# Beginning the transfers that regroup attention weights on POOL's queue, both ways together

## The chip, the cores and the metric

The kernel runs on one core of one Trainium2 chip. The metric is the device time of one execution in microseconds; the time of the kernel before is the median of three runs. One further execution was profiled, and every row of a trace below comes from that one.

## What is computed

Two transformer blocks of width 1024 are applied one after the other to 512 tokens, all in float32. The first has two layers, each with three attentions side by side: `forgetting_attention` (A, 4 heads), `dilated_mixture_attention` (B, 6 heads) and a banded attention with sinks (C, 6 query heads, 2 key heads). The second has two layers as well. The first of them holds the differential attention with a relative bias, and both hold a cross attention to 256 memory rows and an MLP.

```python
def reference(x, norm_g, w_in, ..., mlp_w2_2):
    x = first_block(x, norm_g, w_in, b_forget, sinks, w_br_a, w_br_b, w_br_c, w_out, final_norm_g)
    return second_block(x, mem_2, rel_bias_2, ...)

# the differential attention, whose weights are regrouped as those of A, B and C are
a = probs(qa, k1) - lam * probs(qc, k2)
return jnp.einsum('bhqk,bkhd->bqhd', a.astype(v.dtype), v)

# the cross attention of a layer
p = jax.nn.softmax(s, axis=-1)
o = jnp.einsum('bhsm,bmhd->bshd', p.astype(h.dtype), kv[:, :, 1]).reshape(B, S, D_MODEL)
```

## The kernel before, in words

`schedule` writes one list of steps for the whole program. Each of five functions, one per engine, walks that list and issues what of it belongs to its engine. So the place of a step in the list is its place in every engine's queue, and there is no other scheduler. Semaphores tie the engines together.

**Products.** Each float32 product is taken as three fp32r products of high and low parts (`tensor_program`, L2118 to L2120). The weights come from HBM in pieces of up to 128x1040 into a ring of four buffers `t_raw` (the step `fetch`, L2063, issued by SP). ACT rounds a piece to `t_whi` (L2261, four buffers), and DVE takes the rest to `t_wlo` (L2434, three buffers). The fetch of piece j+4 waits until DVE has made the low part of piece j, since it overwrites that piece's buffer.

**Attention.** `attention` works through units, each two heads (or one head's two maps) by 128 or 256 queries. Matmuls of the projections that come next (`gens_B`, `gens_C`, `gens_D`, `fill_E`, `fill`) are drawn in between by `drive`, in a fixed ratio. A unit goes: scores on PE (L2135), mask and maximum on DVE, exponents on ACT, division and write of the weights into a block by ACT (L2362, L2398) or, in the differential attention, by DVE (L2694); then the regrouping; then the values on PE (L2146). The weights have queries on the partitions, and the values need keys there.

**The regrouping** is made of three steps. `far_out` (L2079) writes the block to the HBM scratch `far` in one DMA, 128 partitions by 4 pieces. `far_in` (L2085) reads it back in four DMAs, each filling 32 partitions with 4 pieces. `turn_near` (L2701) then transposes 32x32 squares on DVE. One such journey, out and back, will be called a **trip**. There are 42 in A, B and C of the two layers (`t_Tb`), 12 in the differential attention (`t_UP`), and 8 in the first cross attention (`t_E`); 310 DMAs in all. Two scratch buffers alternate (`w` is 0 or 1): the way out waits until the trip two before it has landed in full (`back`). The way back waits until the way out has landed, and for a free buffer. The block is a ring of one buffer, so the next unit's weights cannot be written before the way out has landed.

**SP's queue.** All DMAs are issued by SP (`sync_program`), one after the other in the order of the list: the fetches of weights, the trips, and the swaps of halves for the rotary embedding (L2074). A waiting instruction holds up all that is behind it. `send_away` puts `far_out` in the list one `flush` after the weights, and `come` puts `far_in` one `flush` further, so that fetches and swaps come to stand between them.

**POOL's queue** (`gpsimd_program`) holds only the ten window sums of the pooling (L2101), which all lie between the last trip of block one and the first of the differential attention.

Of the kernel before, what the change touches and what calls it, by code (L numbers as in the profile page):

```python
# [95 lines left out]
class Signals:  # L96
# [5 lines left out]
    def mark(self, name, n=0, by=1):  # L102
        sem = SEMAPHORE.get(name, name)
        self.count[sem] = self.count.get(sem, 0) + by
        self.value[name, n] = self.count[sem]
        return sem, by

    def at(self, name, n=0):
        return name, 0
# [49 lines left out]
def schedule(T, A, plan, apart=()):  # L159
# [5 lines left out]
    def emit(name, **f):  # L165
        n = ids[name] = ids.get(name, -1) + 1
        s = Rec(f, name=name, id=n)
        steps.append(s)
        return s
# [20 lines left out]
    def gcol(name, t=0):  # L190
        return gv[:, GV[name] + t:GV[name] + t + 1]
# [14 lines left out]
    if not dry:  # L206
        at = 0
# [153 lines left out]
    def later(f, n=1):  # L361
        late.append(f if n == 1 else lambda: later(f, n - 1))
# [202 lines left out]
    def send_away(u):  # L565
        n = u["tiles"]
        src, ready = u["far"]
        w, k = moved[0] % 2, moved[0] // 2
        moved[0] += 1
        far = A["far"][w][:, :, 0:32 * n]  # L570

        def go():
            emit("far_out", w=w, k=k, dst=far.rearrange("j p c -> p j c"),
                 src=src[:, 0:128 * n].rearrange("p (j c) -> p j c", j=4), after=ready, back=back[w])
            blocks.give(src, (f"far{w}", k))
            later(come)

        def come():
            dst, free = grouped.take()
            emit("far_in", w=w, k=k, free=free,  # L580
                 pairs=[(dst[32 * j:32 * j + 32, 0:128 * n].rearrange("p (i c) -> p i c", i=4),
                         far[j].rearrange("(i a) c -> a i c", i=4)) for j in range(4)])
            back[w] = f"near{w}", (k, 3)
            u["near"] = dst, back[w]

        later(go)
# [270 lines left out]
    for m in range(8):  # L857
        s = emit("norm_hi", dst=P0.hi[:, m, :], src=X[:, m, :], col=gcol("norm0", m), after=c_x[m], gain=c_gv)
# [1193 lines left out]
def sync_program(e, steps, at, mark):  # L2052

    sent = 0
    for s in steps:
        if s.name == "load":
            for k in s.after:
                e.wait_ge(*at(*k))
            e.dma_start(s.dst, s.src).then_inc(*mark(f"load{s.n}", by=16))
        elif s.name == "fetch":  # L2060
            for k in s.after:
                e.wait_ge(*at(*k))
            e.dma_start(s.dst, s.src).then_inc(*mark(f"raw{s.j % NRAW}", s.j, by=16))  # L2063
        elif s.name == "fetch_cut":
            e.dma_start(s.dst, s.src).then_inc(*mark(f"cut{s.j}{s.k}", by=16))
        elif s.name == "rope":
            e.wait_ge(*at("rope_sin", s.n))
            for k in s.bfree:
                e.wait_ge(*at(*k))
            if s.before is not None:  # L2070
                e.wait_ge(*at(*s.before))
            for q in range(4):
                to, of = 32 * (q ^ 1), 32 * q
                e.dma_start(s.b[to:to + 32, :], s.u[of:of + 32, :]).then_inc(*mark(f"swap{s.n % 3}", (s.n, q), by=16))  # L2074
        elif s.name == "far_out":
            e.wait_ge(*at(*s.after))
            if s.back is not None:
                e.wait_ge(*at(*s.back))
            e.dma_start(s.dst, s.src).then_inc(*mark(f"far{s.w}", s.k, by=16))  # L2079
        elif s.name == "far_in":  # L2080
            e.wait_ge(*at(f"far{s.w}", s.k))
            for k in s.free:
                e.wait_ge(*at(*k))
            for j, (dst, src) in enumerate(s.pairs):
                e.dma_start(dst, src).then_inc(*mark(f"near{s.w}", (s.k, j), by=16))  # L2085
        elif s.name == "send":
            e.wait_ge(*at("scaled", s.id))
            e.dma_start(s.dst, s.x).then_inc(*mark("sent", s.id, by=16))
            sent = s.id
    e.wait_ge(*at("sent", sent))  # L2090


def gpsimd_program(e, steps, at, mark):

    for s in steps:
        if s.name == "pool_in":
            e.wait_ge(*at("pool_in", s.g))
            for i, (dst, a, b) in enumerate(s.adds):
                if i:
                    e.wait_ge(*at("window", (s.g, i - 1)))  # L2100
                e.tensor_tensor(dst, a, b, ALU.add).then_inc(*mark("window", (s.g, i)))  # L2101


def tensor_program(e, steps, at, mark, T):
# [839 lines left out]
def build_program(nc, A, pack):  # L2944
    from contextlib import ExitStack

    with ExitStack() as ctx:
# [9 lines left out]
        for program in (sync_program, gpsimd_program):  # L2957
            program(Counting(), steps, signals.at, signals.mark)
# [12 lines left out]
        @block.sync  # L2971
        def _(e):
            sync_program(e, steps, at, mark)
# [9 lines left out]
        @block.gpsimd  # L2983
        def _(e):
            gpsimd_program(e, steps, at, mark)
# [96 lines left out]
```

## Time and profile before

| | |
|---|---|
| median of three runs | 2223.2 us (2221.88 to 2223.98) |
| profiled execution, its own time | 2222.34 us |
| its span in the trace | 2220.3 us |
| TensorE matmul busy | 2199.0 us, 99% of the span |
| DVE busy | 1454.9 us, 66% |
| ACT busy | 975.7 us, 44% |
| POOL busy | 14.5 us, 1% |
| 16 DMA engines, mean share | 39% |

A busy PE here means that a matmul was under way by the trace; matmuls are pipelined, and one with 512 columns starts every 0.23 us. Times in the trace count from the start of the span. Stretches that matter: block one's attentions from 60 to 310 us and from 480 to 745 us, the differential attention from 925 to 1025 us, the first cross attention from 1090 to 1180 us.

### The profile page before, as it was taken

What the parts mean: (1) busy time and instruction counts of PE and PEld (TensorE: products, weight loads), DVE (VectorE), ACT (ScalarE), POOL (GpSimd) and SP (SyncE); (2) the same over time, 40 slices, a digit from 0 to 9 for tenths busy, and PEclk for the clock granted to TensorE, in tenths of its full rate; (3) what the DMA queues carried; (4) which work ended last, traced back from release to release, by engine and by line L of the source; (5) the groups of instructions that cost most, each with busy time, mean ns of one, the idle gap of its engine ahead of it and who ended that gap; (6) DMA issues with size and microseconds to landing.
All of it is one profiled execution on the core that took longest, in us unless ns stands there. A gap on an engine that the chain in (4) does not pass through costs nothing.

```text
span 2220.3 us, 31738 instructions
## 1 busy us (share of the span) xinstructions
PE 2199.0 (99%) x12112; PEld 1860.7 (84%) x12112; DVE 1454.9 (66%) x2448; ACT 975.7 (44%) x1676; POOL 14.5 (1%) x14
## 2 busy tenths in 40 slices
PE   9999999999999999999999999999999999999998
PEld 7877788888778888888898889998888888899997
DVE  5866565557656567686665777776755657776775
ACT  5445533334445334364553544443322435444444
POOL 0000000000000000200000000000000000000000
PEclk9999999999999999999999999999999999999999
DMA  5565443335644333465354333333233213233331
GB/s 201 164 186 156 146 129 109 104 125 180 185 135 152 116 101 115 125 176 147 114 154 132 95 95 96 114 96 105 88 99 96 89 48 105 88 102 97 99 112 55
DMA packets 136694, 268.14 MB, mean 121 GB/s; under 512 B 21773, under 2 KB 79931, under 8 KB 136160
## 3 DMA queue, kind: packets, MB, share of 16 engines
q1 hardware_dynamic: 136544, 266.13, 39.3%
q8 instruction: 96, 1.57, 0.3%
q14 instruction: 54, 0.44, 0.1%
HBM read 235.37 MB, written 26.77 MB: 118 GB/s over the span
## 4 chain that ended last, share of the span: by engine, by line
PE 70%; DVE 3%; ACT 1%; issue 1%; DMA 1%; POOL 1%; SPq 0%; DVEq 0%; POOLq 0%; ACTq 0%
PE ps L2118 22%; PE ps L2120 22%; PE ps L2119 22%; PE ps L2146 1%; PE ps L2135 1%; DVE t_wlo L2434 1%; POOL t_UP L2101 1%; DMA far<-t_UP 0%; DVE t_UP L2694 0%; PE ps L2170 0%; DVE t_Tb L2662 0%; PE ps L2158 0%; PE ps L2160 0%; PE ps L2159 0%; PE ps L2172 0%
## 5 line engine op out<-in xcount | busy, mean ns | idle before, releaser
L2118 PE MATMUL ps<-t_P0H,t_whi 128*128 128x512 f32 (+1 forms) x1568 | 590.6, 377 | 3.8 <-DVE t_P0L L2479 1.9
L2119 PE MATMUL ps<-t_P0L,t_whi 128*128 128x512 f32 (+1 forms) x1568 | 584.4, 373 | 0.0
L2120 PE MATMUL ps<-t_P0H,t_wlo 128*128 128x512 f32 (+1 forms) x1464 | 552.8, 378 | 0.0
L2434 DVE TENSOR_TENSOR t_wlo<-t_raw,t_whi 128x1024 fp32r<-128x1024 f32 (+2 forms) x289 | 342.7, 1186 | 44.7 <-PE ps L2120 32.2
L2261 ACT ACTIVATE t_whi<-t_raw 128x1024 fp32r<-128x1024 f32 (+2 forms) x295 | 300.8, 1025 | 153.6 <-PE ps L2120 152.1
L2118 PEld LDWEIGHTS ps<-t_P0H,t_whi 128*128 128x128 f32 x1568 | 295.2, 188 | 73.1 <-issue 16.4
L2119 PEld LDWEIGHTS ps<-t_P0L,t_whi 128*128 128x128 f32 x1568 | 294.9, 188 | 56.2 <-issue 1.0
L2120 PEld LDWEIGHTS ps<-t_P0H,t_wlo 128*128 128x128 f32 x1464 | 275.2, 188 | 54.7
L2118 PE MATMUL ps<-t_P1H,t_whi 128*128 128x512 f32 (+1 forms) x548 | 210.0, 383 | 1.6 <-DVE t_P1L L2819 1.0
L2119 PE MATMUL ps<-t_P1L,t_whi 128*128 128x512 f32 (+1 forms) x548 | 208.5, 380 | 0.0
L2120 PE MATMUL ps<-t_P1H,t_wlo 128*128 128x512 f32 (+1 forms) x524 | 201.1, 384 | 0.0
L2119 PE MATMUL ps<-t_P1L,t_MH 128*128 128x512 f32 x384 | 150.7, 393 | 0.0
L2120 PE MATMUL ps<-t_P1H,t_ML 128*128 128x512 f32 x384 | 150.6, 392 | 0.0
L2118 PE MATMUL ps<-t_P1H,t_MH 128*128 128x512 f32 x384 | 150.2, 391 | 0.0
L2831 DVE TENSOR_TENSOR t_X<-ps,t_X 128x512 f32<-128x512 f32 (+1 forms) x136 | 88.8, 655 | 74.0 <-PE ps L2120 73.9
L2268 ACT ACTIVATE t_whi<-t_raw 128x1024 fp32r<-128x1024 f32 x72 | 75.8, 1055 | 109.4 <-DVE t_raw L2449 109.4
L2118 PEld LDWEIGHTS ps<-t_P1H,t_whi 128*128 128x128 f32 x548 | 103.2, 188 | 22.9 <-DVE t_P1L L2819 1.2
L2119 PEld LDWEIGHTS ps<-t_P1L,t_whi 128*128 128x128 f32 x548 | 103.1, 188 | 20.8 <-issue 0.2
L2120 PEld LDWEIGHTS ps<-t_P1H,t_wlo 128*128 128x128 f32 x524 | 98.4, 188 | 20.9
L2414 ACT ACTIVATE t_TMP<-t_TMP 128x512 f32<-128x512 f32 x64 | 40.2, 628 | 136.6 <-DVE t_TMP L2827 136.6
L2287 ACT ACTIVATE t_P0H<-t_X,t_gv 128x512 fp32r<-128x512 f32 x56 | 40.3, 725 | 113.7 <-DVE t_X L2600 100.7
L2342 ACT ACTIVATE t_Tb<-t_Tb,t_ST 128x128 f32<-128x128 f32 (+3 forms) x96 | 51.6, 539 | 86.7 <-DVE t_ST L2670 73.0
(348 smaller groups left out, 3880.4 us busy)
## 6 DMA issues: line engine op xcount, KB each, us to landing
t_raw<-in_wts SPq DMA_DIRECT2D x362, 512.0 KB, 3.6
far<-t_Tb SPq DMA_DIRECT2D x26, 384.0 KB, 3.1
far<-t_Tb SPq DMA_DIRECT2D x16, 512.0 KB, 3.4
t_PTX<-far SPq DMA_DIRECT2D x64, 96.0 KB, 3.5
t_raw<-in_wts SPq DMA_DIRECT2D x16, 384.0 KB, 3.2
t_QKV<-far SPq DMA_DIRECT2D x32, 128.0 KB, 2.8
t_raw<-in_wts SPq DMA_DIRECT2D x13, 256.0 KB, 2.8
t_PTX<-far SPq DMA_DIRECT2D x24, 128.0 KB, 4.0
```

Of the source, the lines that this page charges most:

```text
L2101: e.tensor_tensor(dst, a, b, ALU.add).then_inc(*mark("window", (s.g, i)))
L2118: e.matmul(s.out, s.sh, s.mh, start=s.first, stop=False, skip_group_check=again)
L2119: e.matmul(s.out, s.sh, s.ml, start=False, stop=False, skip_group_check=again)
L2120: i = e.matmul(s.out, s.sl, s.mh, start=False, stop=s.end, skip_group_check=again)
L2135: i = e.matmul(bank[:, o:o + n], q, k, start=True, stop=True)
L2261: e.activation(s.dst, s.raw, ACT.Copy).then_inc(*mark("hi", s.j))
L2268: e.activation(s.hi, s.src, ACT.Copy).then_inc(*mark("part_hi", s.id))
L2287: e.activation(s.dst, s.src, ACT.Copy, scale=s.col).then_inc(*mark("norm_hi", s.id))
L2342: i = e.activation(t[:, o:o + n], t[:, o:o + n], ACT.Exp, bias=s.s[:, 4 + c + k:5 + c + k], accum_out=s.s[:, 8 + c + k:9 + c + k])
L2414: e.activation(s.t, s.t, ACT.Square).then_inc(*mark("relu_square", s.id))
L2434: e.tensor_tensor(s.dst, s.raw, s.hi.bitcast(F32), ALU.subtract).then_inc(*mark("lo", s.j))
L2831: e.tensor_tensor(s.x, s.bank, s.x, ALU.add).then_inc(*mark("add_x", s.id))
```

## The change

The two steps of a trip move from `sync_program` to `gpsimd_program`, and `come` is called at once where it was put off by a `flush`, so that the way back stands directly behind the way out in the list. Nothing else is changed; PE, DVE and ACT have the same instructions in the same order.

```diff
             blocks.give(src, (f"far{w}", k))
-            later(come)
+            come()
@@ def sync_program
-        elif s.name == "far_out":
-            e.wait_ge(*at(*s.after))
-            if s.back is not None:
...
+def gpsimd_program(e, steps, at, mark):
+
+    for s in steps:
+        if s.name == "pool_in":
...
+        elif s.name == "far_out":
+            e.wait_ge(*at(*s.after))
+            if s.back is not None:
+                e.wait_ge(*at(*s.back))
+            e.dma_start(s.dst, s.src).then_inc(*mark(f"far{s.w}", s.k, by=16))
+        elif s.name == "far_in":
+            e.wait_ge(*at(f"far{s.w}", s.k))
+            for k in s.free:
+                e.wait_ge(*at(*k))
+            for j, (dst, src) in enumerate(s.pairs):
+                e.dma_start(dst, src).then_inc(*mark(f"near{s.w}", (s.k, j), by=16))
```

SP's queue at the start of the differential attention, before (a row is one instruction, or several alike with their count: line, DMA, what is written from what, the shape):

```order
L2063 DMA t_raw<-in_wts 128x1024 x3
L2079 DMA far<-t_UP 128x4x96
L2063 DMA t_raw<-in_wts 128x1024
L2085 DMA t_UP<-far 32x4x96 x4
L2079 DMA far<-t_UP 128x4x96
L2085 DMA t_UP<-far 32x4x96 x4
L2063 DMA t_raw<-in_wts 128x1024
L2079 DMA far<-t_UP 128x4x128
L2063 DMA t_raw<-in_wts 128x1024
L2085 DMA t_UP<-far 32x4x128 x4
```

In the changed kernel SP's queue has only fetches there (thirteen in a row), and these rows stand on POOL, behind the window sums:

```order
+L2090 TENSOR_TENSOR t_UP<-t_UP 128x512 x10
+L2095 DMA far<-t_UP 128x4x96
+L2101 DMA t_UP<-far 32x4x96 x4
+L2095 DMA far<-t_UP 128x4x96
+L2101 DMA t_UP<-far 32x4x96 x4
+L2095 DMA far<-t_UP 128x4x128
+L2101 DMA t_UP<-far 32x4x128 x4
```

So a trip is held up by no fetch any more and holds up none, and a way out stands behind the whole trip before it. In the changed kernel L2095 is the way out, L2101 the way back and L2090 the window sums.

## Rows read from the trace of the kernel before

**Rows 1.** The page's first part: busy time of each engine
```profile
span 2220.3 us, 31738 instructions
PE 2199.0 (99%) x12112; PEld 1860.7 (84%) x12112; DVE 1454.9 (66%) x2448; ACT 975.7 (44%) x1676; POOL 14.5 (1%) x14
```

**Rows 2.** Busy time by stretches of the program; the last columns are clock, DMA share, GB/s
```profile
60.00:125.00 65.00, 62.31 (x403) 52.51 (x403) 51.03 (x95) 26.35 (x54) 0.00 (x0) 1.00 0.59 178
925.00:1025.00 100.00, 94.88 (x701) 85.71 (x700) 79.45 (x227) 61.26 (x123) 0.00 (x0) 1.00 0.59 169
1090.00:1180.00 90.00, 89.94 (x642) 84.26 (x641) 56.54 (x92) 47.73 (x90) 0.00 (x0) 1.00 0.52 153
```

**Rows 3.** Who waited for whom, 925 to 1025 us: total us, times, longest
```profile
DVE t_UP L2694 <- DMA far<-t_UP: 4.0, 2, 2.0
PE ps L2146 <- DVE t_E L2778: 2.8, 2, 1.7
PE ps L2118 <- DVE t_wlo L2434: 1.9, 1, 1.9
DVE t_PTb L2701 <- DMA t_UP<-far: 0.8, 1, 0.8
```

**Rows 4.** The chain that ended last, 925 to 1025 us: start, us, what
```profile
929.94 3.32 DMA far<-t_UP
...
937.64 0.58 DVE t_PTb L2701
...
941.78 1.24 DVE t_wlo L2434
943.15 0.47 PE ps L2118
```

**Rows 5.** Way out L2079, then way back L2085, 925 to 1025 us: ns of issue; landing
```profile
L2079 SPq DMA_DIRECT2D far<-t_UP x12: 370/382/383, 929.9 to 1010.0; - x12
DMA to landing us min/median/max: 2.2/3.1/5.7
...
L2085 SPq DMA_DIRECT2D t_UP<-far x48: 302/432/441, 933.3 to 1014.2; - x48
DMA to landing us min/median/max: 1.7/2.5/3.8
```

**Rows 6.** POOL's own work, L2101, whole span: ns min/median/max
```profile
L2101 POOL TENSOR_TENSOR t_UP<-t_UP x10: 1040/1156/1952, 898.6 to 922.0; 128x512 f32<-128x512 f32 x10
```

**Rows 7.** Way back L2085, whole span: ns of issue, min/median/max
```profile
L2085 SPq DMA_DIRECT2D t_E<-far x32: 313/432/2001, 1097.9 to 1170.1; - x32
```

**Rows 8.** Timeline: ACT's last write of a block (L2362), DVE's turn (L2701)
```profile
533.80 0.71 ACT L2362 ACTIVATE t_Tb<-t_TbX,t_ST 128x512 f32<-128x512 f32 x1
543.33 1.25 DVE L2701 STREAM_TRANSPOSE t_M<-t_M 128x1024 f32<-128x1024 f32 x1 [1.54 <-DMA t_M<-far]
```

**Rows 9.** The same two steps (L2398, L2701) of the last cross attention trip
```profile
1163.02 0.91 ACT L2398 ACTIVATE t_E<-t_Tb,t_ST 128x256 f32<-128x256 f32 x2 [1.24 <-DVE t_ST L2804]
1172.19 0.71 DVE L2701 STREAM_TRANSPOSE t_PTb<-t_E 128x512 f32<-128x512 f32 x1 [4.33 <-DMA t_E<-far]
```

**Rows 10.** Timeline 925 to 950 us: DVE's write of the block, then SP's queue
```profile
939.17 1.14 DVE L2694 SCALAR_TENSOR_TENSOR t_UP<-t_Tb,t_ST 128x128 f32<-128x128 f32 x4 [0.63 <-ACT t_Tb L2352]
948.03 0.88 DVE L2694 SCALAR_TENSOR_TENSOR t_UP<-t_Tb,t_ST 128x128 f32<-128x128 f32 x3 [2.04 <-DMA far<-t_UP]
943.03 0.35 SPq L2063 DMA_DIRECT2D t_raw<-in_wts  x1
943.48 0.38 SPq L2079 DMA_DIRECT2D far<-t_UP  x1
```

**Rows 11.** SP's waits, whole span: total us, times, longest; and ACT's for a fetched piece (L2261)
```profile
SPq L2079 <- ACT t_Tb L2362: 71.5, 28, 6.5
SPq L2085 <- DMA far<-t_Tb: 42.3, 22, 3.8
...
  DMA t_raw<-in_wts: 1.3, 3
```

More of the change, by code:

```diff
@@ L2074, in sync_program @@
                 e.dma_start(s.b[to:to + 32, :], s.u[of:of + 32, :]).then_inc(*mark(f"swap{s.n % 3}", (s.n, q), by=16))
-        elif s.name == "far_out":
-            e.wait_ge(*at(*s.after))
-            if s.back is not None:
[L2078 to L2085, printed above, removed]
         elif s.name == "send":
```

## The prediction

> **What bounds the kernel now.** I read the page's first part, then busy time by stretches, then the waits and the chain inside the stretches that hold trips. PE is busy for 2199.0 of 2220.3 us [rows 1], and it runs the same matmuls after the change. So all a faster trip can give is some of PE's idle time there: 2.7 us between 60 and 125 us, 5.1 us between 925 and 1025 us, and 0.1 us between 1090 and 1180 us [rows 2]. What can be lost has no such limit. A trip that lands late stops DVE at the turn, and DVE also makes the low parts of the weights for PE. The place to look at is the differential attention, since DVE is busy there for 79.5 of 100 us [rows 2] and has little room to catch up. PE's stalls there end with DVE's work: 2.8 us on values and 1.9 us on a low part [rows 3]. Just before that 1.9 us the chain runs way out (3.32 us), way back, turn [rows 4]: this first trip is on the path already, for its turn waits 0.8 us for the landing [rows 3].
>
> **What goes away.** (1) SP loses 310 issues. They stood beside other work. SP waited 71.5 us for weights to be written and 42.3 us for ways out to land [rows 11] with fetches queued behind it, but ACT waited for a fetched piece only three times, 1.3 us in all [rows 11]. Freed fetches are covered by the four-buffer ring; I count nothing. (2) A trip no longer queues behind a fetch. The clearest case: DVE has written a block at 939.17 + 1.14 = 940.3 us, but SP issues it at 943.48, right behind a fetch issued at 943.03. DVE then waits 2.04 us for that way out to land before it may write the next block [rows 10]. On POOL the issue can be 3.2 us earlier. I count **-2.0 us**.
>
> **What is added.** POOL must issue one DMA out and four back per trip. No row shows a DMA issued by POOL, so its price is bounded. Below: SP's issue, 0.38 us out and 0.43 us back [rows 5]. Above, for the way back: the longest single issue that SP shows, 2.0 us [rows 7]. Above, for the way out: its whole time from issue to landing, 3.1 us [rows 5], as if writing out the transfer's parts took as long as moving them. For the way back I take 1.04 us, POOL's shortest instruction on a full tile [rows 6], the nearest row of that engine. The way out has 512 runs of memory (128 x 4) against 128 in a piece of the way back (32 x 4), so I take the middle of its two ends, (0.38 + 3.1) / 2 = 1.75 us.
>
> The rest of a landing: the shortest way out landed 2.2 us after its issue began [rows 5], 1.8 without the issue; I take 1.9. For the way back the median is 2.5 us, less 0.43 makes 2.1; with pieces spaced further apart I take 2.0. A trip from block written to landed is then 1.75 + 1.9 + 4 x 1.04 + 2.0 = **9.8 us**, and it holds POOL's queue for all but the last 2.0, **7.8 us**, as the way back waits in the queue for the way out.
>
> The Trainium skill ("DMA: Bandwidth & Descriptors", Latency and other measured facts) puts the first byte of a POOL transfer at about 1 us and that of an SP transfer at about 0.6 us. By these figures alone the two legs would lose some 0.8 us a trip; no run so far shows it.
>
> **Where 9.8 us is late.** From the block written to the turn there are now:
> - first trip of the differential attention: 929.9 to 937.64, 7.7 us [rows 4]. Late by **2.1 us**, in full, since it is on the path.
> - last forgetting trip of layer two: 534.5 to 543.33, 8.8 us [rows 8]; its twin of layer one, read the same way, 9.5 us. Late by 1.0 and 0.3 us, 1.3 in all. I count half, **0.6 us**, DVE being busy there for 51.0 of 65 us [rows 2].
> - last cross attention trip: 1163.9 to 1172.19, 8.3 us [rows 9], late by 1.5; two more of its eight, read the same way, have 8.9 and 9.1 us and are late by 0.9 and 0.7. DVE's wait of 4.33 us there [rows 9] goes with 0.1 us lost on PE [rows 2]. Of 3.1 us I count half, **1.6 us**.
> - the other 57 trips, read the same way, have 10 to 23 us and are covered; if POOL's cost eats that cover, the heavy rival below holds.
>
> **The queue itself.** The 12 ways out of the differential attention are issued from 929.9 to 1010.0 us [rows 5], one per 7.28 us. A trip would hold POOL for 7.8 us. So POOL becomes the slowest stage there, and each of the 11 intervals grows by 0.5: **+5.7 us**. In the cross attention the cadence is (1164.0 - 1095.3) / 7 = 9.8 us, the first and last way out being those of its eight trips, and in block one's attentions it is longer still, so nothing piles up there. POOL's window sums end before 925 us [rows 2, 6] and collide with nothing.
>
> Sum: -2.0 + 2.1 + 0.6 + 1.6 + 5.7 = +8.0 us. I add 1 us for trips of the differential attention between the first and the last whose room is 10 to 12 us and which start behind a late one: **+9 us**. The profiled execution took 2222.34 us, so the next would take 2231.3; the median of the runs stands 0.9 higher, which gives **2232 us** for it. What a measurement here can tell from no change is about 0.2%, 4.4 us.
>
> **Rivals.**
> 1. *Hidden.* If POOL issues either way for at most 0.7 us, a trip takes 0.7 + 1.9 + 2.8 + 2.0 = 7.4 us, under the tightest 7.7, and holds POOL for 5.4 of 7.28 us. Nothing is late and the -2.0 stands: 2221 us, no change that can be told. For it: PE is 99% busy [rows 1] and most trips have much room. Against: a software path on an engine whose shortest full tile instruction takes 1.04 us [rows 6]. The Trainium skill (same page, Anatomy of one DMA) says that a DMA issued by POOL costs about 2.0 us plus 1 us per 436,000 bytes, and that writing its descriptors is a small part. By that rule a way out of 192 KB would land after an estimated 2.5 us and the overlapping ways back in little over 2.1 us, and this rival would win; the page is the main thing that speaks for it. 22%.
> 2. *Faster.* The same cheap issue, and the freed order also gives PE back its stalls: the 1.9 us on a low part, behind which stands the trip chain, and the 2.8 us on values [rows 3]. 2223.2 - 4.7 = 2218.5 us. It decides where a trip lands before 7.7 us and SP's fetches in front of it were what held DVE. Against: DVE's 79.5% [rows 2] stays, and only one of these waits leads back to a trip. 11%.
> 3. *Heavy.* The way out costs POOL its upper bound, 3.1 us. A trip is then 11.2 us and holds POOL for 9.2: in the differential attention 11 x (9.2 - 7.28) = 21 us and 3.5 for the first trip, in the cross attention 2.9 late at the last trip and some 6 over the others, in block one 1.7 + 2.7 at the two tight trips, in all some 37 less 2: 2258 us. With 1.5 us for each way back as well it would pass 2300. The Trainium skill ("SBUF — State Buffer", Who interferes with whom) adds a way to it: POOL writes descriptors through a port that some DVE instructions lock. No row here shows such a lock. 27%.
> 4. *Nothing happens*, since waits tie the trips to the same moments. The queues do change, and the 3.2 us behind a fetch [rows 10] shows that the order bound somewhere. 2%, at 2223 us.
>
> **Numbers.** The forecast, +4.5 to about +20 us, has 38%; hidden 22%, faster 11%, heavy 27%, nothing 2%. Faster by over 0.2% gets 0.11, within it 0.24, and slower 0.65. The range reaches from the better part of the faster case, 2219, up through the forecast into the heavy case, 2278, past its 2258 as that rests on one bound of two.
>
> **What would show it.** POOL's DMA rows: about 1.75 us (way out) and 1.04 us (way back). At the first trip of the differential attention the turn waits some 3 us, not 0.8. The 12 ways out there are spread over 86 us, not 80. DVE's waits for `far` landings at L2701 grow from 2 or 3 to about ten, and PE's idle time between 925 and 1025 us from 5 to about 12 us. Between 1180 us and the end nothing should change. The prediction is wrong if POOL's DMAs cost under 0.7 us, or if the turns wait but PE does not, DVE having caught up in its idle fifth; and wrong the other way if the way out costs over 2.5 us.

## The result, and the profile after

The changed kernel took **2245.0 us** (median of four runs, 2237.38 to 2247.43) against 2223.5 us (2221.88 to 2223.98) for the kernel before on the same chip: a ratio of 1.0091, 95% interval 1.0073 to 1.0110. That is slower by 21.5 us, about 0.9%. The forecast was 2232 us, 9 us slower, with a range of 2219 to 2278.

The profiled execution took 2237.38 us, the shortest of the four, with a span of 2235.5 us; its trace explains 15.2 us of the loss and not the whole 21.5. More on this under the unexpected.

The page's first part, changed kernel (it answers to [rows 1]):

```profile
span 2235.5 us, 31738 instructions
PE 2205.3 (99%) x12112; PEld 1866.3 (83%) x12112; DVE 1455.1 (65%) x2448; ACT 974.9 (44%) x1676; POOL 197.7 (9%) x324
```

DVE and ACT have the same work. POOL has 183 us more, all of it issuing DMAs. PE is busy 6.3 us longer with the same matmuls, and idle 8.9 us longer. By stretches (columns as in [rows 2]):

```profile
60.00:125.00 65.00, 63.39 (x402) 54.08 (x401) 49.85 (x94) 26.65 (x55) 17.88 (x30) 0.97 0.59 178
925.00:1025.00 100.00, 88.21 (x622) 79.02 (x623) 74.61 (x219) 56.70 (x116) 32.95 (x57) 0.98 0.48 143
1090.00:1180.00 90.00, 90.00 (x601) 82.49 (x600) 58.29 (x89) 46.62 (x89) 21.39 (x36) 1.00 0.49 146
```

In the differential attention PE idles 11.8 us where it idled 5.1, and the DMA engines are less busy, 0.48 where it was 0.59: the transfers are not what is overloaded. The same way out, seen in both traces, dates the loss. A negative number would be a gain:

| way out | before | changed | later by |
|---|---|---|---|
| first of block one | 62.42 | 63.03 | 0.6 |
| first of its second layer | 486.01 | 487.22 | 1.2 |
| first of the differential attention | 929.94 | 932.46 | 2.5 |
| last of it | 1010.01 | 1024.79 | 14.8 |
| first of the cross attention | 1095.27 | 1107.79 | 12.5 |
| end of the span | 2220.3 | 2235.5 | 15.2 |

So 10.0 us arise between the first way out of the differential attention and the first of the cross attention, 2.7 us behind that, and 2.5 us before. The waits of 925 to 1025 us (it answers to [rows 3]; the stage now runs beyond this stretch):

```profile
POOL t_UP L2101 <- DMA far<-t_UP: 33.9, 11, 4.5
...
POOL far L2095 <- issue: 25.9, 11, 4.1
DVE t_UP L2694 <- DMA far<-t_UP: 14.3, 7, 3.1
...
PE ps L2118 <- DVE t_wlo L2434: 5.6, 2, 2.9
...
PE ps L2146 <- DVE t_E L2778: 3.3, 1, 3.3
...
PE ps L2206 <- DVE t_lam L2497: 2.9, 1, 2.9
...
DVE t_PTb L2701 <- DMA t_UP<-far: 3.1, 5, 1.4
```

DVE waits 14.3 us for ways out to land before it may write the next block, where it waited 4.0, and PE waits for DVE. The second row is new, and no term of the prediction stands for it: POOL idles 25.9 us before 11 of the 12 ways out, and "issue" means that the profile shows nothing it waited for. Each of those 11 is ready by the program's semaphores: its block is written, and the trip two before it has landed. The chain that ended last (it answers to [rows 4]) runs through these idle times, trip after trip:

```profile
932.46 2.76 DMA far<-t_UP
935.22 0.31 issue
935.53 1.46 POOL t_UP L2101 x3
937.17 0.55 POOL t_UP L2101
937.72 1.91 issue
939.64 2.58 DMA far<-t_UP
```

And the DMAs themselves (they answer to [rows 5]):

```profile
L2095 POOL DMA_DIRECT2D far<-t_UP x12: 759/768/774, 932.5 to 1024.8; - x12
DMA to landing us min/median/max: 2.6/3.8/4.9
...
L2101 POOL DMA_DIRECT2D t_UP<-far x46: 549/549/571, 935.5 to 1029.9; - x46
DMA to landing us min/median/max: 1.9/2.2/4.3
```

POOL needs 0.77 us for a way out and 0.55 us for a piece of the way back, not 1.75 and 1.04. A whole trip's issues are 0.77 + 2.19 = 3.0 us. The 12 ways out are nevertheless spread over 92.3 us, one per 8.4, where they came one per 7.28.

What ends the unexplained idle time can be read off by lining up the landings of the way back's four pieces with the next way out. For the second way out of the program, issued at 73.73, its four predecessors' landings lie 4.79, 2.51, 2.20 and 0.35 us before it; for the third, at 83.25, 1.91, 1.43, 0.94 and 0.35 us. In 42 of the 61 trips that have one before them, the way out starts 0.35 us after the **last** piece has landed; in the other 19 it starts 0.5 us after its block is written. Nothing in the program asks for the first.

### The profile page after: what moved, and what is told of

It is laid out like the page before. It is cut to its first block, busy times and chain, and to the rows that moved or that the text cites. A ratio compares the mean times of both kernels' runs of the same rounds, so it can differ in the third digit from the quotient of the medians.

```text
span 2235.5 us, 31738 instructions
## 1 busy us (share of the span) xinstructions
PE 2205.3 (99%) x12112; PEld 1866.3 (83%) x12112; DVE 1455.1 (65%) x2448; ACT 974.9 (44%) x1676; POOL 197.7 (9%) x324
## 3 DMA queue, kind: packets, MB, share of 16 engines
q8 instruction: 96, 1.57, 0.3%
## 4 chain that ended last, share of the span: by engine, by line
PE 66%; issue 4%; DMA 4%; POOL 3%; DVE 1%; ACT 0%; DVEq 0%; POOLq 0%; ACTq 0%
PE ps L2118 21%; PE ps L2120 21%; PE ps L2119 21%; DMA far<-t_UP 2%; DMA far<-t_E 1%; POOL t_UP L2101 1%; DMA far<-t_Tb 1%; PE ps L2146 1%; POOL t_E L2101 1%; PE ps L2135 1%; POOL t_UP L2090 1%; POOL t_M L2101 0%; PE ps L2160 0%; PE ps L2158 0%; PE ps L2159 0%
## 5 line engine op out<-in xcount | busy, mean ns | idle before, releaser
L2261 ACT ACTIVATE t_whi<-t_raw 128x1024 fp32r<-128x1024 f32 (+2 forms) x295 | 300.3, 1024 | 157.0 <-PE ps L2120 155.6
```

The costliest lines, as they stand in the source:

```text
L2261: e.activation(s.dst, s.raw, ACT.Copy).then_inc(*mark("hi", s.j))
```

## The experiments

Three theories were set against each other. A **run** is a stretch of neighbouring bytes in HBM; **descriptor** stands for what POOL has to write down about one run before it is moved.
- **Theory 1, room.** The place where POOL puts the descriptors of its transfers (`dynamic_dma_scratch_size=1024` bytes in this kernel) holds only so many, and a way out that finds no room waits on POOL.
- **Theory 2, in flight.** POOL begins no way out while another of its transfers is under way. As first written down this holds whatever their size; after experiment 2 it is left for transfers of many runs (512 here) alone.
- **Theory 3, price.** What POOL spends issuing, 3.0 us a trip, is what costs the time, and the waits only show it.

Every ratio below is against the kernel before, on the same chip.

**1. The second edit undone.** Only the queue is changed; `come` is put off again.

```diff
-            come()
+            later(come)
```

> The changed kernel with its second edit undone: the way back is put one flush later in the list, but still goes to POOL. On every engine the instructions stand in the same order as in the changed kernel, since the fetches that came between on SP are on another queue. All theories: the same time as the changed kernel, 2240 to 2248 us, and POOL's way out starts 0.35 us after the landing of the way back before it in some 39 of 61 trips. It also shows how far profiles of one program differ.

Measured: 2240.8 us (2235.62 to 2243.66), ratio 1.0082, interval 1.0069 to 1.0095. The order of the rows on every engine is that of the changed kernel, since POOL's queue has nothing that could come between. The part of the change that puts the way back "directly behind" moves nothing; this is a second measurement of the same program, with the 0.35 us pattern in 43 trips, and the 4 us between the two medians is how much this program scatters.

**2. The scratch in HBM laid out row by row.** A way out then has 128 runs of memory instead of 512; the same bytes move.

```diff
-    A["far"] = nc.dram_tensor("far", (2, 4, 128, 256), _mybir.dt.float32).ap()
+    A["far"] = nc.dram_tensor("far", (2, 128, 1024), _mybir.dt.float32).ap()
@@
-            emit("far_out", w=w, k=k, dst=far.rearrange("j p c -> p j c"),
-                 src=src[:, 0:128 * n].rearrange("p (j c) -> p j c", j=4), after=ready, back=back[w])
+            emit("far_out", w=w, k=k, dst=far, src=src[:, 0:128 * n], after=ready, back=back[w])
```

> The changed kernel with the scratch in HBM laid out row by row (128 rows of 3 or 4 KB), so that the way out is 128 long runs and no longer 512 short ones; bytes, number of DMAs and order are the same. Theory 1 (POOL has room for about 64 runs per DMA engine in flight: 33 out and 36 back, 69 in all, do not fit, so a way out waits for the way back before it to land): now 9 and 36 fit, the 0.35 us pattern goes, a way out starts some 0.5 us after its block is written, the differential attention's ways out spread over 80 to 83 us, and the time is 2223 to 2230 us. Theory 2 (POOL begins no way out while any of its earlier DMAs is in flight, whatever their size): the pattern stays, 2238 to 2246 us. Theory 3 (it is the price of an issue, 0.77 and 0.55 us against 0.38 and 0.43): the pattern may stay or go, the time falls by no more than 62 x 0.4 us of issue, mostly hidden, to 2240 us or so.

Measured: 2221.0 us, ratio 0.9998, interval 0.9989 to 1.0007. The whole loss is gone with all 310 DMAs still on POOL. POOL's longest waits in the whole span:

```profile
POOL far L2095 <- ACT t_Tb L2362: 464.8, 38, 176.9
...
POOL far L2095 <- ACT t_E L2398: 109.4, 8, 79.8
...
POOL far L2095 <- DVE t_UP L2694: 30.3, 9, 6.9
```

A way out now waits only for its block, and in 26 trips it starts while pieces of the trip before are still in flight. POOL spends 0.57 us on it instead of 0.77, and starts it 0.28 us after its block is written, not 0.5; the time lies 2 us below what was expected. Theory 2 as it was written down, "whatever their size", falls with those 26 trips. Narrowed to transfers of many runs it is still alive beside theory 1, since the way out has fewer runs now; theory 3 is nearly dead, as the issues of a trip fell by 0.2 of 3.0 us and the loss by all of it.

**3. The same layout with all DMAs on SP.**

> The kernel before with the same row by row scratch, all trips on SP. No theory of POOL's queue speaks of it: it shows what the layout alone is worth. Four times fewer runs on the way out should land it in 2.3 to 2.8 us instead of 3.1; the first trip of the differential attention is on the path, so 0.5 to 2 us are gained: 2221.5 to 2223 us.

Measured: 2221.9 us, ratio 1.0000, interval 0.9991 to 1.0009. So the layout by itself brings nothing, and experiment 2 is not a loss offset by a gain. A way out of the differential attention lands a median 2.8 us after its issue, where it took 3.1 [rows 5], and nothing is gained by it.

**4. Only the way out on POOL**, the way back on SP at its old place.

> The changed kernel with the way back returned to SP at its old place in the list; only the ways out go to POOL. Theories 1 and 2: POOL's queue never waits for a landing and never has two DMAs in flight, so nothing is held: 2221 to 2226 us, ways out start 0.5 us after the block is written. Theory 3 (price): each way out is 0.4 us dearer and the first byte later: 2223 to 2228 us, so this run alone does not tell them apart; with the run of the row layout it does.

Measured: 2221.6 us, ratio 0.9999, interval 0.9990 to 1.0008. The way out, with its 512 runs and in its old layout, still takes POOL 0.76 us, and POOL waits before it only for a block:

```profile
POOL far L2101 <- ACT t_Tb L2362: 691.7, 42, 183.7
...
POOL far L2101 <- ACT t_E L2398: 147.9, 8, 84.5
POOL far L2101 <- DVE t_UP L2694: 78.1, 12, 9.8
```

(In this kernel L2101 is the way out.) There are 62 ways out, and 42 + 8 + 12 = 62 waits for blocks.

**5. Only the way back on POOL**, the way out on SP at its old place.

> Only the ways back stand on POOL; the ways out are SP's as before, at their old place in its queue. The theory of full room: a way back wants 36 of 64 places, and the one before it has landed by then except where two trips follow within a few microseconds; so POOL's pieces wait for the way out of their own trip and hardly ever for room. Ways out start, as in the kernel before, 0.03 us after their block is written or behind a fetch. Time 2220 to 2225 us. If it were instead the way back on POOL (its four pieces of 0.55 us against 0.43) that costs the changed kernel its time, it would be 2235 us or more.

Measured: 2220.6 us, ratio 0.9994, interval 0.9985 to 1.0004. Either half alone is free; the loss needs both on one queue. That is what theory 1 wants (the two halves share one place), and what theory 3 can't give, since the way back's 2.2 us are the larger part of the price.

**6 to 8. The room alone.** First the changed kernel's program with more bytes for descriptors, every instruction of it the same. A small table moves to another place in SBUF to make room. It moves in the same way with 1088 and 1152 bytes (below), and with 1088 the loss is there, so the move is not what removes it.

```diff
-    for n, s in (("MRC", [128, 2]), ("MRB", [128, 256]), ("lam", [128, 168]), ("ic", [128, 64])):
+    for n, s in (("MRC", [128, 2]), ("MRB", [128, 256]), ("lam", [128, 168])):
         put(n, s)
+    put("ic", [128, 64], offset=kt + 6208)
@@
-    nc = _bacc.Bacc("TRN2", target_bir_lowering=False, num_devices=1, dynamic_dma_scratch_size=1024)
+    nc = _bacc.Bacc("TRN2", target_bir_lowering=False, num_devices=1, dynamic_dma_scratch_size=1280)
```

> The changed kernel with short ways out (512 runs) as they were, and only the space that POOL's DMAs have in each SBUF partition raised from 1024 to 1280 bytes (a small table moves elsewhere to make room for it). If POOL holds 16 bytes per run and per engine there, 64 become 80 and 33 + 36 = 69 fit. Theory 1: the 0.35 us pattern goes though the way out still costs 0.77 us, the differential attention's ways out spread over 80 to 84 us, time 2220 to 2227 us. Theory 2 (a way out of many runs is only begun when nothing of POOL's is in flight): the pattern stays, 2238 to 2246 us.

Measured: 2223.2 us, ratio 1.0004, interval 0.9995 to 1.0012. **This settles it for the changed kernel:** same instructions, same layout, same issue times, and some 20 us less. POOL's timeline at the start of the differential attention, with 1280 bytes (start, us, instruction, and in brackets the idle time before it with its releaser):

```profile
929.42 0.77 POOL L2095 DMA_DIRECT2D far<-t_UP  x1 [7.06 <-DVE t_UP L2694]
932.31 2.29 POOL L2101 DMA_DIRECT2D t_UP<-far  x4 [2.11 <-DMA far<-t_UP]
934.59 0.76 POOL L2095 DMA_DIRECT2D far<-t_UP  x1
937.46 2.29 POOL L2101 DMA_DIRECT2D t_UP<-far  x4 [2.11 <-DMA far<-t_UP]
939.74 0.77 POOL L2095 DMA_DIRECT2D far<-t_UP  x1
```

The same piece of the changed kernel, with 1024 bytes:

```profile
932.46 0.77 POOL L2095 DMA_DIRECT2D far<-t_UP  x1 [7.15 <-DVE t_UP L2694]
935.53 2.19 POOL L2101 DMA_DIRECT2D t_UP<-far  x4 [2.29 <-DMA far<-t_UP]
939.64 0.76 POOL L2095 DMA_DIRECT2D far<-t_UP  x1 [1.92 <-issue]
942.53 2.19 POOL L2101 DMA_DIRECT2D t_UP<-far  x4 [2.13 <-DMA far<-t_UP]
946.64 0.76 POOL L2095 DMA_DIRECT2D far<-t_UP  x1 [1.92 <-issue]
```

Three trips begin within 10.3 us with 1280 bytes and within 14.2 with 1024. Over the whole span 29 ways out start while pieces of the trip before are in flight, where the changed kernel has none. The number of runs is the same in both, so theory 2 falls in its narrowed form too, and theory 3 with it.

How much room is wanted? The layout of experiment 2 was run with 640 bytes, then with 768, in place of 1024.

> The row by row layout on POOL with that space cut to 640 bytes, 40 runs per engine: 9 out and 36 back are 45 and do not fit. Theory 1: the pattern comes back, a way out starts 0.35 us after the landing of the way back before it wherever that lands after the block is written, and the time goes up to 2232 to 2245 us. Theory 2: no pattern, 2219 to 2225 us, as with 1024 bytes.

Measured: 2238.5 us, ratio 1.0076, interval 1.0063 to 1.0089. The pattern of 0.35 us is back in 41 trips, though a way out has only 128 runs. This goes against the narrowed theory 2 from the other side: few runs, and the wait is there.

> The same with 768 bytes, 48 runs per engine: 45 fit. Theory 1 in its exact form (16 bytes a run, one more per DMA): no pattern, 2219 to 2226 us. If the count is off by a few runs, or if two trips of ways back count together, the pattern shows here as well.

Measured: 2222.5 us, ratio 1.0000, interval 0.9990 to 1.0009, and no way out waits for room.

**9. The way out in two DMAs of 64 partitions**, with 1024 bytes.

```diff
-            e.dma_start(s.dst, s.src).then_inc(*mark(f"far{s.w}", s.k, by=16))
+            for h in (slice(0, 64), slice(64, 128)):
+                e.dma_start(s.dst[h], s.src[h]).then_inc(*mark(f"far{s.w}", s.k, by=16))
```

> The changed kernel with each way out in two DMAs of 64 partitions, 17 runs per engine each. In flight: 36 of the way back, then 17 make 53 of 64, then 17 more make 70. Theory 1: the first half starts within about 0.5 us of the block's writing; the second waits. If room is given back piece by piece it waits only for the first piece of the way back; if POOL waits until all is empty, for the last, and then for the first half too. Time: a little under the changed kernel's in the first case, 2230 to 2240 us; 2240 to 2255 us in the second, since the halves land one after the other. Theory 2: both halves wait, and the time is 2240 to 2250 us.

Measured: 2232.4 us, ratio 1.0049, interval 1.0032 to 1.0067. POOL's timeline, with L2102 the way back and L2096 the two halves:

```profile
68.84 0.56 POOL L2102 DMA_DIRECT2D t_PTX<-far  x1
69.39 0.63 POOL L2096 DMA_DIRECT2D far<-t_Tb  x1
73.54 0.62 POOL L2096 DMA_DIRECT2D far<-t_Tb  x1 [3.52 <-issue]
```

The first half goes at once, with all four pieces of the way back in flight (they land at 70.97, 71.41, 71.78 and 73.19). The second waits until 73.54, again 0.35 us after the last of them. It doesn't wait for the first half, which lands at 73.58. That is no accident: in 39 trips the second half starts 0.35 us after the last piece has landed, and in 35 of these the first half is still under way. So room is asked for transfer by transfer, and half the way out fits where the whole doesn't. The expectation had two branches, and neither came true whole: the first half doesn't wait, and the second doesn't go with the first piece, whose 9 places would have been enough for the 6 it lacked.

**10 to 12. The edge.** Take a place, the room of one descriptor, as 16 bytes, so that 1024 bytes are 64 places for each of the 16 DMA engines. Let a DMA want its runs divided by 16, and one more. A way out of 512 runs then wants 33, a piece of the way back (128 runs) 9, four of them 36: together 69. Row by row the way out wants 9, together 45. Three runs put the size just below and just above.

> The changed kernel with 1088 bytes of scratch for POOL's transfers, where it has 1024: 68 places for each DMA engine by the count of 16 bytes to a place. A way out (32 runs per engine and one) and the way back before it (four times 8 and one) want 33 + 36 = 69. The theory of full room with exactly this count says: one place short, so every way out that follows closely begins 0.35 us after the last piece of the way back before it has landed, as in the changed kernel, and the time is 2236 to 2246 us. If a transfer wanted only its 32 and 8 places without the extra one (64 in all, which 1024 bytes would have held), or if the room were reckoned otherwise, the ways out would start 0.5 us after their block is written and the time would be 2221 to 2225 us.

Measured: 2239.1 us, ratio 1.0078, interval 1.0061 to 1.0095. One place short, and all of the wait is there; POOL's waits in the whole span hold

```profile
POOL far L2095 <- issue: 132.7, 40, 5.4
```

where the changed kernel has

```profile
POOL far L2095 <- issue: 126.0, 39, 5.3
```

> The same with 1152 bytes: 72 places, 69 wanted. The theory of full room says that nothing waits: ways out start 0.5 us after their block is written, even while pieces of the way back are under way, way out still 0.77 us on POOL, time 2220 to 2225 us. If the room wanted is larger than counted (between 72 and the 80 that were enough), the 0.35 us pattern stays and the time is 2236 to 2246 us.

Measured: 2223.9 us, ratio 1.0007, interval 0.9998 to 1.0016; the same wait is down to

```profile
POOL far L2095 <- issue: 1.1, 4, 0.3
```

> The kernel with the scratch in HBM laid out row by row and 704 bytes: 44 places, where a way out (8 runs per engine and one) and the way back before it (36) want 45. The theory of full room says: one short, the 0.35 us pattern is there and the time is 2236 to 2243 us, as with 640 bytes. Without the extra place per transfer (40 wanted) nothing would wait and the time would be 2219 to 2225 us, as with 768 bytes.

Measured: 2242.5 us, ratio 1.0090, interval 1.0075 to 1.0105, with the pattern in 41 trips.

| layout | wanted | places | way out held by landings | time, us |
|---|---|---|---|---|
| by pieces | 69 | 64 (1024 bytes) | yes | 2245.0, 2240.8 |
| by pieces | 69 | 68 (1088) | yes | 2239.1 |
| by pieces | 69 | 72 (1152) | no | 2223.9 |
| by pieces | 69 | 80 (1280) | no | 2223.2 |
| by rows | 45 | 40 (640) | yes | 2238.5 |
| by rows | 45 | 44 (704) | yes | 2242.5 |
| by rows | 45 | 48 (768) | no | 2222.5 |
| by rows | 45 | 64 (1024) | no | 2221.0 |

Eight kernels fall on the side that the count gives, and without the one extra place per DMA (64 and 40 wanted) the four with 1024 and 1088 by pieces, 640 and 704 by rows would not. The steps of 4 places leave the extra between 5 and 8 for the five DMAs; one each is the simplest that fits. The 16 bytes can be had from the runs as well: the edge lies between 1088 and 1152 bytes by pieces and between 704 and 768 by rows, so the 384 runs more of a way out, 24 per engine, want 320 to 448 bytes, 13 to 19 each.

**What stays open.** Why POOL waits for the last piece. In the changed kernel 28 places are free beside the way back, and the first piece to land gives 9, enough for 33; with 68 places one missing place would do. In both, the start follows the last landing. That POOL looks for room only when all its transfers have landed is ruled out by experiment 9, where the second half starts with the first under way. That the room of the four pieces is given back together would fit every run, and none tests it. Open as well is why a way out lands later in the changed kernel: in the differential attention a median 3.8 us after its issue, where it is 2.8 with 1280 bytes.

No version beat the kernel before by more than the measurement is uncertain; the best medians, 2220.6 to 2221.0 us, have intervals around 1.

## Why the prediction was right, and where it was not

**The direction, and the place.** It said that POOL's queue would become the slowest stage of the differential attention and that DVE, kept waiting by late trips, would stop PE. That is what happened, though DVE waited at the block and not, as forecast, at the turn: 10.0 of 15.2 us arise there, against 6.8 predicted (-2.0 + 2.1 + 5.7 + 1), and ways out are 8.4 us apart, against 7.8. But two of its terms were wrong in opposite directions, and that the sum came close is luck. With the measured issues in its own sum, a trip would hold POOL for 0.77 + 1.9 + 2.2 = 4.9 us, under the 7.28, nothing would be late, and the forecast would have been the 2221 us of the *hidden* rival.

**The price of an issue** (1.75 and 1.04 us) was over-sized: 0.77 and 0.55. POOL's full tile instructions were the nearest row, and it was not near: a piece of the way back costs half of the shortest of them. By the prediction's own sign of being wrong, DMAs under 0.7 us, the way back meets it and the way out just does not. The rule of the Trainium skill weighed there ("DMA: Bandwidth & Descriptors", Anatomy of one DMA: writing descriptors is a small part) was right on this: 0.77 us of issue in a landing after 3.8 (median). Its estimated 2.5 us from issue to landing stands beside 2.6 at the least.

**What a trip holds** was under-sized, at 7.8 us against 8.4. The step "it holds POOL's queue for all but the last 2.0" failed: it put the last landing, and the wait for room behind it, at nothing. Measured, for the trip issued at 932.46: 0.77 issue, 1.99 to the landing, 0.31 until POOL goes on, 2.19 for four pieces (with a short gap), 1.57 to the last landing, 0.35: 7.18 us until the next may start. Ways out that land after up to 4.9 us make it 8.4 on average. With room, a trip holds POOL for 5.2 us (929.42 to 934.59), under the 7.28, and nothing piles up. So the condition of the *hidden* rival (issues of at most 0.7 us) was all but met with 0.77 and 0.55, and its 5.4 us was about right. It lost all the same, to a resource that none of the four rivals named. It is what the kernel would have done with 128 more bytes.

**The first trip, +2.1 us:** did not occur. Block written at 931.96, turn at 939.38:

```profile
939.38 0.58 DVE L2701 STREAM_TRANSPOSE t_PTb<-t_UP 128x384 f32<-128x384 f32 x1 [0.52 <-DMA t_UP<-far]
942.30 1.14 DVE L2694 SCALAR_TENSOR_TENSOR t_UP<-t_Tb,t_ST 128x128 f32<-128x128 f32 x4 [1.93 <-DMA far<-t_UP]
```

That is 7.4 us, within the 7.7. I had said the turn would wait 3 us; it waits 0.52, less than before. The second row shows what hurt instead: the **next** block, which waits 1.93 us because the second way out was held for room until 939.64. PE's stalls grew behind this, on low parts from 1.9 to 5.6 us. DVE's waits at the turn stayed few (five in the stretch), where I had forecast about ten: the lateness went through the block, one buffer deep, not through the turn.

**-2.0 us for SP's fetch ahead of a way out:** the mechanism is real and worth nothing. With 1280 bytes the third way out goes at 939.74, 3.7 us earlier than in the kernel before, and DVE's wait of 2.04 us at the block [rows 10] is gone. PE still waits 1.5 us for a low part there, and the span is 2220.8 us against 2220.3. The *faster* rival falls with it. The first trip still stands on the chain before that low part (way out at 929.42, turn at 936.36), now 0.7 us shorter, and the stall shrank from 1.9 to 1.5 us; PE's wait on values is as long as before (2.7 us, 2.8 before).

**The last trips.** In block one's second layer (0.6 us counted for both layers) and in the cross attention (1.6 counted), the turns that answer to [rows 8, 9]:

```profile
547.12 1.25 DVE L2701 STREAM_TRANSPOSE t_M<-t_M 128x1024 f32<-128x1024 f32 x1 [5.12 <-DMA t_M<-far]
...
1186.13 0.71 DVE L2701 STREAM_TRANSPOSE t_PTb<-t_E 128x512 f32<-128x512 f32 x1 [6.16 <-DMA t_E<-far]
```

Both were found by the right test (a trip's room against its length), with waits of 5.12 and 6.16 us where they were 1.54 and 4.33. PE waited 1.6 us for the first turn. From the first way out of the cross attention to the end 2.7 us are lost. Four of the seven later ways out are held there too (they start 0.35 us after a last landing), but little piles up, as the prediction's "cadence 9.8 us" said: the last way out is 12.7 us later than before, the first 12.5. The rest arises after it. The last turn comes 13.9 us later than before, and right behind it PE waits for a low part, where the kernel before has no such wait (1090 to 1200 us):

```profile
PE ps L2118 <- DVE t_wlo L2434: 1.9, 1, 1.9
```

Then the granted clock is 0.87 and 0.70 in the next two stretches of 4 us.

Two readings of the prediction were off by little: 56 trips were left, not 57, and one of them, the last of the differential attention, had 9.5 us from block to turn and not 10; and in *heavy* the tighter trip of block one is late by 11.2 - 8.8 = 2.4 us, not 2.7.

**Heavy** rested on a way out of 3.1 us; it was 0.77. The port lock that the Trainium skill describes ("SBUF — State Buffer", Who interferes with whom) is not seen in any run: POOL's 62 ways out in the changed kernel stay within 0.76 to 0.90 us beside a DVE that is busy 65% of the time, and no other kernel has a longer one.

**The size.** The median went 13 us beyond the forecast. By the profiled execution the miss is 6 (2237.4 against 2231.3): 3.2 in the differential attention, and the rest around it. The other 7 lie between this execution and the median.

## What to carry to other kernels

A queue on POOL has a length, measured in descriptors, and a DMA of many small runs takes more of it. In this kernel a DMA wants one place for every 16 of its runs and one more, and there are as many places as the scratch size in bytes over 16. Add up what is in flight and the next DMA; where that doesn't fit, POOL stops until the transfers ahead that hold the room have landed, and so holds everything behind. The count is known for the two layouts tried here alone. The profile names no releaser for it ("issue" ahead of a DMA on POOL, ending a constant 0.35 us after some landing); lining up starts with earlier landings finds it. When moving DMAs to another queue, price the hold of the queue (from a start to the next possible start), not the issue: here 3.0 us of issues were a hold of 8.4 us.

## What was not expected of the hardware

- POOL's descriptor room, as above: by the count it is 64 places for 1024 bytes, and one missing place costs as much as five (2239.1 and 2240.8 to 2245.0 us).
- In the changed kernel POOL issues 0.31 us after a landing that it waits for, and when held for room, 0.35 us; after a block is written, 0.5 us. The waits for a semaphore are not the same in every kernel: with the same instructions and 1152 bytes POOL takes 0.48 us after a landing, with 1280 bytes 0.41 us after a block, by rows 0.28. Where no fetch stood ahead, SP issued 0.02 us after the block.
- The price of an issue on POOL grows slowly with runs: 0.55 us for 128 runs in a piece of the way back, 0.57 for 128 in a way out, 0.63 for 256, 0.77 for 512.
- The clock. PE's busy time grew by 6.3 us with the same matmuls. In stretches of 4 us of the changed kernel (columns as in [rows 2]):

```profile
944.00:948.00 4.00, 1.72 (x8) 1.45 (x9) 3.66 (x10) 3.76 (x10) 1.48 (x3) 1.00 0.33 67
948.00:952.00 4.00, 4.00 (x23) 3.40 (x22) 2.46 (x8) 1.95 (x4) 1.10 (x2) 1.00 0.85 293
...
968.00:972.00 4.00, 0.71 (x7) 0.55 (x5) 3.97 (x10) 0.00 (x0) 1.30 (x2) 1.00 0.72 183
972.00:976.00 4.00, 4.00 (x24) 4.00 (x23) 3.22 (x12) 3.82 (x12) 0.27 (x1) 0.57 0.68 205
...
1000.00:1004.00 4.00, 1.45 (x13) 1.24 (x11) 1.42 (x4) 0.89 (x3) 1.19 (x3) 1.00 0.42 166
1004.00:1008.00 4.00, 3.64 (x22) 2.38 (x22) 4.00 (x8) 3.82 (x5) 1.76 (x3) 1.00 0.64 168
...
1020.00:1024.00 4.00, 1.35 (x11) 1.18 (x11) 3.41 (x7) 1.57 (x3) 2.17 (x4) 0.97 0.18 49
1024.00:1028.00 4.00, 3.94 (x22) 3.64 (x22) 3.99 (x7) 2.33 (x4) 0.76 (x1) 0.61 0.81 218
```

PE has four stalls of 2.7 to 3.3 us here, at 943, 968, 1001 and 1021 us. After two of them the granted clock is 0.57 and 0.61 for the next 4 us, so mostly the lower of its two levels (1.2 instead of 2.4 GHz), though PE is at work again; after those at 943 and 1001 us it isn't. By an estimate from these rows the two stretches lose 4 x 0.43 + 4 x 0.39 = 3.3 us, a third of the 10.0. With 0.60 from 116 to 120 us and the 0.87 and 0.70 behind the cross attention it makes 6.6 us, about what PE's busy time grew by. In the kernel before, whose longest stall in the stretch is 1.9 us, the clock is 1.00 throughout it. So a wait that PE sees costs more than its length, and not each time. The runs' mean clocks point the same way, 0.993 to 0.995 in the changed kernel's four and 0.997 to 0.999 in 74 runs of the kernel before; the profiled one, with 0.995, took 2237.4 us, the others, with 0.993 and 0.994, 2244.4 to 2247.4. A thousandth of 2240 us is 2.2 us, so the clock is a part of the 7 us that lie between the profiled execution and the median, and not all; the rest of it was not traced.
